# A two-layer step with routed experts on one core: the last three chunks' rows stay in SBUF and are placed by products, the further chunks run in pairs in the middle

## What is computed

```python
u = x * (1 + scale1) + shift1
y, k, v = token_mixer(u, p, lam_init, rope, ctx_kv)
x = layer_norm(ALPHA * x + gate1 * y, p['ln1_g'], p['ln1_b'])
u = x * (1 + scale2) + shift2
x = layer_norm(ALPHA * x + gate2 * hier_moe(u, p), p['ln2_g'], p['ln2_b'])
...
h = silu(einsum('nd,edf->nef', t, p['w_gate'])) * einsum('nd,edf->nef', t, p['w_up'])
y = einsum('nef,efd->nd', h * comb[:, :, None], p['w_down'])
```

## Time and profile before

| what | us |
|---|---|
| median of 3 runs (1164.85 to 1168.12) | 1165.8 |
| the profiled execution | 1164.11 |
| its span, first to last instruction | 1162.3 |
| PE busy | 928.0 |
| DVE busy | 368.5 |
| ACT busy | 234.0 |
| POOL busy | 172.4 |

### The profile page before, as it was taken

One profiled execution on the slowest core, in us unless ns is written; L12 is line 12 of the kernel. 1 busy time (PEld: TensorE's weight loads), 2 busy tenths in 40 slices (PEclk: granted clock), 3 DMA queues, 4 the chain that ended last, 5 costly groups with the idle time before them and its releaser, 6 DMA issues.

```text
span 1162.3 us, 13769 instructions
## 1 busy us (share of the span) xinstructions
PE 928.0 (80%) x5214; PEld 535.7 (46%) x5214; DVE 368.5 (32%) x887; ACT 234.0 (20%) x575; POOL 172.4 (15%) x203
## 2 busy tenths in 40 slices
PE   3899988984999877775789989898599887777542
PEld 2356455543555534342345546554455543433222
DVE  0158462154211111110547845116311111111052
ACT  1200265052111110111230036306011110101023
POOL 5000000002232222211020000000232222221100
PEclk8899989996999999999789999999799999999976
DMA  9962162266999999999932227038699999996521
GB/s 367 378 252 92 57 249 93 100 277 241 387 414 414 414 413 413 411 411 380 363 120 109 108 91 288 3 131 334 251 397 412 416 413 412 411 413 255 226 110 54
DMA packets 72831, 321.86 MB, mean 277 GB/s; under 512 B 12974, under 2 KB 17286, under 8 KB 48448
## 3 DMA queue, kind: packets, MB, share of 16 engines
q1 hardware_dynamic: 57680, 294.14, 63.5%
q0 software_dynamic: 14224, 20.57, 5.0%
q10 hardware_dynamic: 864, 6.29, 1.4%
HBM read 320.93 MB, written 23.59 MB: 296 GB/s over the span
## 4 chain that ended last, share of the span: by engine, by line
PE 53%; SPq 22%; DMA 12%; DVE 8%; issue 2%; ACT 2%; ACTq 0%; DVEq 0%; POOLq 0%; POOL 0%
PE ps L751 13%; PE ps L979 9%; SPq L541 8%; SPq L543 7%; PE ps L927 7%; SPq L548 6%; PE ps L994 4%; DMA arena<-in_w_up 4%; PE ps L754 4%; DMA ring<-in_w_mod 3%; PE ps L713 3%; DMA arena<-y_pairs 2%; PE ps L909 2%; PE ps L914 2%; PE ps L987 1%
## 5 line engine op out<-in xcount | busy, mean ns | idle before, releaser
L979 PE MATMUL ps<-ring,tail 128*64 128x256 f32 x1728 | 201.2, 385 | 35.3 <-DMA ring<-in_w_up 33.4
L979 PEld LDWEIGHTS ps<-ring,tail 128*64 128x64 f32 x1728 | 135.4, 139 | 115.8 <-DMA ring<-in_w_up 55.1
L751 PE MATMUL ps<-uT,ring 128*128 128x384 f32 x448 | 152.2, 497 | 8.5 <-ACT uT L1093 8.2
L1627 DVE TENSOR_TENSOR arena<-arena,ps 128x128 f32<-128x128 f32 x68 | 19.5, 287 | 382.6 <-ACT arena L1249 382.6
L751 PEld LDWEIGHTS ps<-uT,ring 128*128 128x128 f32 x448 | 86.3, 194 | 67.2 <-issue 11.0
L1249 ACT ACTIVATE arena<-ps 128x128 f32<-128x128 f32 x68 | 18.8, 277 | 484.9 <-PE ps L979 484.9
L646 POOL DMA_INDIRECT y_pairs<-tail,row_idx x64 | 64.6, 1009 | 341.6 <-PE ps L987 297.7
L994 PE MATMUL ps<-ring,krow 128*64 128x512 f32 x432 | 104.6, 601 | 2.6 <-issue 1.3
L641 POOL DMA_INDIRECT arena<-u_rows,row_idx x66 | 67.5, 1023 | 42.3 <-issue 20.0
L713 PE MATMUL ps<-ring,sT 128*32 128x512 f32 (+1 forms) x512 | 52.8, 555 | 21.0 <-DMA ring<-in_w_mod 21.0
L1379 DVE SCALAR_TENSOR_TENSOR arena<-arena,dw 128x414 f32<-128x414 f32 x118 | 67.6, 645 | 0.0
(11 more groups left out here) (243 smaller groups left out, 959.1 us busy)
## 6 DMA issues: line engine op xcount, KB each, us to landing
ring<-in_w_gate SPq DMA_DIRECT2D x54, 1024.0 KB, 17.8
ring<-in_w_up SPq DMA_DIRECT2D x54, 1024.0 KB, 23.6
ring<-in_w_down SPq DMA_DIRECT2D x54, 1024.0 KB, 23.5
ring<-in_w_mod SPq DMA_DIRECT2D x12, 3072.0 KB, 12.7
arena<-in_w_gate SPq DMA_DIRECT2D x14, 1024.0 KB, 17.6
arena<-in_w_up SPq DMA_DIRECT2D x14, 1024.0 KB, 23.2
arena<-in_w_down SPq DMA_DIRECT2D x14, 1024.0 KB, 23.5
ring<-in_w_mod SPq DMA_DIRECT2D x6, 2048.0 KB, 15.7
```

Source lines behind the costliest of these rows:

```text
L751: last = mm(ps[:, n % 4, 0:T], slot[s][:, k, c:c + P], uT[:, k, :], start=(k == 0), stop=(k == KD - 1))
L979: last = mm(ps[W * half:W * (half + 1), b, 0:2 * P].rearrange("p (j f) -> p j f", j=2), xc[:, b, k, :], gate_up_w[s][:, :, k, half * P:(ha ...
```

## The change

**Start.** Of the table of constants only the first 256 columns load ahead of everything; the rest loads behind the first projection slot.

**Further chunks in the middle.** 31 experts' chunks are unrolled. The 32nd expert's chunk and all further chunks form a list that runs in a loop after the first 20, two in a turn, on slots 3 and 4, with doubled buffers; the list is filled up to an even number. Then the other 11 chunks follow. The last chunks use slots 0 to 3 alone.

**The last three chunks** (28 to 30) are not scattered. Their rows in `y_pairs` are set to zero by three puts at the start of the stage; the rows of 28 and 29 are stacked in one tile, 64 partitions each (`down_stacked`), those of 30 stay in `yrow`. Placing matrices (row, token) that hold the routing weights are built by DVE and turned by PE before the first chunk (`late_places`). After chunk 30 `late_products` multiplies rows by placing matrices straight into the PSUM tiles from which z is made, and the sums of the pair rows are added onto them by products with the identity. POOL issues the loads of the pair rows when chunk 27 is stored.

**Norm.** The gain is applied in the scaling itself (`xT = centred * gain * 1/root`); the bias is folded into the modulation's shift (`mod_fold`) and into the next residual. `scale_x` of the second residual moves into chunks 20 to 27. Of the modulation products that follow a norm, two or three k-tiles move between the sums and the sums of squares; the next layer's first ones come after the norm.

```diff
+NS = NE - 1
+SPLIT = 20
+PLACE = [i if i < SPLIT else i + 2 for i in range(NS)]
+PUT = NS - 3
+SLOT_AT = [(FIRST_SLOT + p) % XRING for p in range(27)] + [0, 1, 2, 3, 1, 0]
...
-            sp.dma_start(cst[:], consts).then_inc(s_cst.sem, 16)
+            sp.dma_start(cst[:, 0:first], consts[:, 0:first]).then_inc(s_cst.sem, 16)
...
+                with sp.Fori(0, turns, 2) as r:
+                    for p in range(2):
...
+                        sp.wait_ge(e_gate_up.sem, before + (r + p + 1))
+                        load_gate_up(LOOP_SLOT[p], ds(e, 1), e_gate_up_loaded[p])
...
+                        sp.wait_ge(e_down.sem, before + (r + p + 1))
+                        load_down(LOOP_SLOT[p], ds(e, 1), e_down_loaded[p])
...
+                for i in range(PUT, NS):
+                    put(row_idx[:, CHUNKS + i:CHUNKS + i + 1], zero_rows, zeros_put)
...
+                    for p in range(2):
+                        pool.wait_ge(e_rows_loaded[p].sem, (before + (r + 2 * l + 4)) * 8)
+                        pool.wait_ge(e_stored[p].sem, (before + (r + 2)) * 8)
+                    pool.sem_inc(e_free.sem, 2)
+                for i in range(SPLIT + 2, SPLIT + 4):
+                    fetch_chunk(i)
...
+                for t in range(NT):
+                    pool.dma_start(yk[:, t, :], y_pairs.rearrange("(t q r) n -> t q (r n)", t=NT, r=4)[t]).then_inc(y_loaded[t].sem, 16)
...
+                        if which == 0:
+                            mod_product(l, 2, 7, range(2))
+                        elif l + 1 < DEPTH:
+                            mod_product(l + 1, 0, 7, range(MOD_K))
...
+                def down_stacked(b, c, s, sig):
+                    for f in range(2):
+                        for half in range(2):
+                            last = mm(ps[W * c:W * (c + 1), 3 + half, :], hT[:, b, f * W:(f + 1) * W],
+                                      down_w[s][:, f, half * 512:(half + 1) * 512],
+                                      start=(f == 0), stop=(f == 1), tile_position=(0, W * c))
...
+                def late_products(m):
+                    h, n = m // 4, m % 4
+                    mm(ps[:, n, 0:T], ystack[:, m * P:(m + 1) * P], late_place[:, 0, :], start=True, stop=False)
+                    mm(ps[:, n, 0:T], yrow[W * h:W * (h + 1), 0, n * P:(n + 1) * P], late_place[W * h:W * (h + 1), 1, :],
+                       start=False, stop=False)
+                wait(y_rows, l, NS)
+                for m in range(4):
+                    late_products(m)
                 wait(y_sum, l, NT)
                 for m in range(KD):
-                    if m >= 4:
-                        wait(z_ready, l, KD + m - 3)
                     for t in range(NT):
-                        last = tr(ps[:, m % 4, t * P:(t + 1) * P], ysum[:, t, m * P:(m + 1) * P], ident)
+                        last = mm(ps[:, m % 4, t * P:(t + 1) * P], yk[:, t, m * P:(m + 1) * P], ident,
+                                  start=False, stop=(t == NT - 1))
                     last.then_inc(y2_ready.sem, 1)
+                    if m + 4 < KD:
+                        wait(z_ready, l, KD + m + 1)
+                        late_products(m + 4)
                     if m >= 1:
                         layer_norm(1, m - 1)
                 layer_norm(1, KD - 1)
+                if l + 1 < DEPTH:
+                    mod_product(l + 1, 0, 7, range(MOD_K, KD))
+                    mod_turn(l + 1, 0, 6, 0)
...
+                wait(y_stored[0], l, SPLIT // 2)
+                wait(y_stored[1], l, SPLIT // 2)
+                with act.Fori(0, turns, 2) as r:
...
-                        v.tensor_tensor(uT[:, m, :], uT[:, m, :], ln_t[:, 0, :], ALU.mult).then_inc(normed.sem, 1)
+                        v.scalar_tensor_tensor(xT[:, m, :], uT[:, m, :], vcol(l, g0, m), ln_t[:, 0, :], ALU.mult,
+                                               ALU.mult).then_inc(normed.sem, 1)
```

More of the change, by code:

```diff
@@ L511, in _ @@
                 else:
-                    sp.wait_ge(e_down.sem, before + 1)
+                    wait(down_done, l - 1, NS, alone=True)
                 load_slot(0, [(slot[0][:, :, POOL:SLOT_COLS], cols(w_in, c0, c0 + 2 * CONV, 0, KD)),
@@ new lines, in _ @@
+                for i in range(SPLIT + 2, SPLIT + 4):
+                    fetch_chunk(i)
+                for i in range(SPLIT, PUT):
+                    if i + XBUFS < NS:
+                        wait(x_turned, l, i + 1, alone=True)
+                        fetch_chunk(i + XBUFS)
+                    put_chunk(i)
+                wait(y_stored[0], l, PUT // 2)
+                wait(y_stored[1], l, PUT // 2)
+                wait(zeros_put, l, 3)
+                wait(down_done, l, max(i for i in range(NS) if SLOT_OF[i] == RING) + 1, alone=True)
@@ new lines, in main_chunks @@
+                def main_chunks(first, end):
+                    main_x(first)
+                    main_x(first + 1)
+                    if first == 0:
+                        late_places()
+                    main_gate_up(first)
+                    for i in range(first, end):
+                        b = i % 2
+                        wait(h_ready, l, i + 1)
+                        wait(hT_ready, l, i - 1)
+                        tr(ps[:, 2 + 5 * b, 0:P], hrow[:, b, :], ident).then_inc(h_turned.sem, 1)
+                        if i + 2 < end:
+                            main_x(i + 2)
+                        s = SLOT_OF[i]
+                        wait(down_loaded[s], l, SLOT_USE[i])
+                        wait(hT_ready, l, i + 1)
+                        wait(y_rows, l, i if i >= PUT else i - 1)
+                        if i < 2:
+                            wait(late_ready, l, 2)
+                        if PUT <= i < NS - 1:
+                            down_stacked(b, i - PUT, s, down_done)
+                        else:
+                            down(b, s, down_done)
+                        if i + 1 < end:
+                            main_gate_up(i + 1)
@@ L1280, in _ @@
+                main_chunks(SPLIT, NS, turns)
+                squares_root(1)
                 if l + 1 < DEPTH:
                     mod_rows_out(l + 1, 0, 7)
-                squares_root(1)
-                new_x("ln2", 1, x_new, (l + 1, 1), SH1, SC1, u_act if l + 1 < DEPTH else None)
+                    new_u(1, (l + 1, 1), SH1, SC1, u_act)
+            for m in range(0, KD, 2):
+                wait(normed, DEPTH - 1, KD + m + 1)
+                fn(uT[:, m, :], xT[:, m, :], ID, bias=vcol(DEPTH - 1, "ln2_b", m)).then_inc(x_out.sem, 1)
@@ new lines, in _ @@
+                wait(h_turned, l, SPLIT)
+                with dve.Fori(0, turns, 2) as r:
+                    for p in range(2):
+                        dve.wait_ge(e_turned.sem, before + (r + (p + 1)))
+                        copy_x(p, e_copied)
+                    for p in range(2):
+                        dve.wait_ge(e_silu.sem, before + (r + (p + 1)))
+                        hidden(p, e_hidden)
+                        dve.wait_ge(e_hturned.sem, before + (r + (p + 1)))
+                        columns(p, e_columns)
@@ L1671, in _ @@
                 residual_norm(1)
-                new_x("ln2", 1, x_new_dve, (l + 1, 1), SH1, SC1, u_dve if l + 1 < DEPTH else None)
-                own.check()
+                if l + 1 < DEPTH:
+                    new_u(1, (l + 1, 1), SH1, SC1, u_dve)
+                    own.check()
+            for m in range(1, KD, 2):
+                wait(normed, DEPTH - 1, KD + m + 1)
+                v.tensor_scalar(uT[:, m, :], xT[:, m, :], vcol(DEPTH - 1, "ln2_b", m), None, ALU.add).then_inc(x_out_dve.sem, 1)
```

525 lines of the change are left out of this document (288 added, 237 removed).

## The result

The changed kernel takes 1181.7 us (median of 4 runs, 1179.8 to 1183.9) against 1165.4 before: a ratio of 1.0136, 95% interval 1.0118 to 1.0153. It is 16.3 us **slower**; 1164.2 was forecast, with a range to 1174. The profiled execution took 1182.6, its span is 1180.8.

The account below looks back on a forecast made before the run. Weights were taken to set the pace, 7.64 us a chunk. Start -2.5, norm -1.6, layer 0 +0.6 and layer 1 +1.9 sum to -1.6: 1164.2 us for the median, range 1150 to 1174.

Parts of the forecast that it names:

- rival B: Residual's stage: PE's waits for DVE in each tile drop the granted clock, +9 us a layer, 1182 us; chance 0.06.
- 22.0 for the stage: Residual's stage, first identity product to last sum of z: takes 22.0 us at full clock.
- Now all but hidden: Before layer 0's residual: pair rows' loads, 15.3 us, and sum end at 124.8, late products at 123.8; 15.9 us lay open before.
- The pace of the stream: Unrolled chunks: three weight loads, 3.146 MB at 412 GB/s, set a pace of 7.64 us a chunk.
- The loop: Middle loop: late fetch of chunk 22 stalls PE from about 32 to 41, leaving it 11 us behind the stream at chunk 30.
- ACT's hold: Loop's start: ACT waits for both y buffers, so the first chunk's SiLU runs 2 us late.
- Late products: After chunk 30: 0.66 us each with issue, eight ahead of the pair rows' sum taking 5.3 us.
- Start and norm: Start: fewer constants ahead of the modulation weights, -2.5 us; norm without separate gain and bias, -0.8 a layer, -1.6 together.
- Behind M both programs do about the same: After each layer's last sum of z, old and new kernels were taken to do about the same work.
- the same work: Norm: modulation products moved around the sums, their weights already in SBUF, lie only at another place; cost 0.
- rival C: Loop: weight stream runs dry with two slots, a chunk costing 12.94 us, adding 10 us, 1174 us; chance 0.13.
- A: Rival: stall behind the loop is short, landings below 5 us, 5.1 us less a layer, 1154 us; chance 0.28.

Follow-up runs that it names:

- e1: Changed kernel, with the next layer's three modulation loads issued only when the pair rows have landed; 1162.4 us, 0.9960 of the kernel before.
- e6: On top of e1, layer 1's pair rows load only behind the last down product; 1179.1 us, 1.0104 of the kernel before.
- e2: Changed kernel, with three k-tiles of modulation products moved ahead of PE's wait for the pair rows' sum; 1168.4 us, 1.0018 of the kernel before.
- e5: As e3 but without placing by products: all 31 chunks scattered, PE turns the sums as before; 1156.0 us, 0.9915 of the kernel before.
- b2: As e5, with the third modulation load held until the pair rows have landed; 1146.8 us, 0.9820 of the kernel before.
- e4: Changed kernel, with the second residual's sums of the previous tile put ahead of PE's wait for z; 1166.9 us, 1.0008 of the kernel before.
- e3: Changed kernel, with x rows of chunks 22 and 23 fetched by the loop's own last turn; 1169.3 us, 1.0021 of the kernel before.

## Why the prediction was wrong

The time came out as rival B, slower at 1182, to which I had given 6 in 100; the range ended below it. That B's figure fits is luck: B had both layers' stages at the low clock, for DVE's wait in each tile, +18. Only layer 0's fell, behind another wait, and the rest came from elsewhere. The profiled time missed by 20.1 us. Gains and losses against the kernel before, by stretch (chunk 19 stands for the start of its gate and up; start and norm of a layer are in the stretch ahead of its chunk 19):

| stretch | forecast | measured |
|---|---|---|
| up to chunk 19 of layer 0 | -3.3 | 0.0 |
| chunk 19 to M, layer 0 | +0.6 | +13.3 |
| M of layer 0 to chunk 19 of layer 1 | -0.8 | +6.2 |
| chunk 19 to M, layer 1 | +1.9 | -1.6 |
| behind M of layer 1 | 0 | +0.6 |

- **The step that failed** is "22.0 for the stage" in layer 0, with full clock taken for granted. In layer 1 the sum was right (22.8 measured). In layer 0 it took 34.9: 12.9 of the 20.1 us. Rows 16 had shown the low clock at this very place behind a wait of 3.08; against it I had argued that the clock came back there "with waits as short" and that PE "comes from dense work now". The waits were not as short: that stage of the kernel before has none above 0.3 us, the new one has 0.9 in four tiles. And PE did come from dense work, but the long wait still came between.
- **"Now all but hidden"**: my sum had the pair rows ready 1.0 us behind the late products. I put 15.3 us on their loads beside the modulation weights; they took 18.7, and PE stood 3.39. That a few us of lateness there would be paid several times over, I did not see: e1 and e6 show it from two sides, and e2's profiled execution from a third. (There is a slip in that sum too: 107.1 + 15.3 is 122.4, not 122.7.)
- **The pace of the stream** was too fast, 7.64 us a chunk; the gathered rows (0.26 MB a chunk) come over the same DMA engines as the weights, and 3.41/0.412 is 8.3. The profile of before has 8.2, in layer 0:

```profile
493.66 3.67 PE L979 MATMUL ps<-ring,tail 128*64 128x256 f32 x32 [1.14 <-DMA ring<-in_w_up]
501.87 3.67 PE L979 MATMUL ps<-ring,tail 128*64 128x256 f32 x32 [1.14 <-DMA ring<-in_w_up]
```

 Chunk 19 thus starts at 420.18 (420.14 before the change) and not at 426.7, and from there to the residual it takes 131.2 us and not 124.8. That the stage began at 551.34, where I had 551.5, is luck: the two errors cancel.
- **The loop** (4.0 of these 6.4 us, with the late products; the rest is the wait for the rows) was right in kind and short in size. ACT's hold cost 3.0 us (2 forecast) and one slow down product 1.65, which I had left out; chunk 22's turning stood 8.76 and 7.54 (8 to 9 forecast).
- **Late products** are 0.84 us apart, not 0.66: 1.4 us for the first eight. Why they are slower than the projections of the same columns was not tried.
- **Start and norm**: the gains came and went. The first projection starts 0.9 earlier and the router 1.0, but the first norm's last sum and the first chunk's gate and up stand where they stood. Timeline of the kernel after:

```profile
40.69 23.11 PE L822 MATMUL ps<-uT,ring 128*128 128x384 f32 x64 [1.67 <-ACT uT L1216]
...
252.83 4.71 PE L1018 MATMUL ps<-uT,router_w 128*36 128x384 f32 x14 [1.31 <-DVE uT L1456]
...
284.95 4.93 PE L1056 MATMUL ps<-ring,tail 128*64 128x256 f32 x32
```

 Against the earlier trace rows: 253.80 and 285.01. The placing matrices' turning (1.49 us) took back what the norm had given. Of -3.3 forecast up to there, nothing was left.
- **"Behind M both programs do about the same"** failed by 6.2 us. M to chunk 19 of layer 1 took 396.0. My numbers give 396.4 (969.9 - 573.5), but only because 7.64 a chunk puts chunk 19 too late in layer 1 as well; in the kernel before it took 389.7. Timeline of before, then of after:

```profile
586.00 1.62 PE L751 MATMUL ps<-uT,ring 128*128 128x384 f32 x2 [6.50 <-ACT uT L1093]
...
962.62 3.67 PE L979 MATMUL ps<-ring,tail 128*64 128x256 f32 x32 [1.16 <-DMA ring<-in_w_up]
```

```profile
586.12 2.78 PE L784 MATMUL ps<-ring,sT 128*32 128x512 f32 x24
...
594.20 4.50 PE L784 MATMUL ps<-ring,sT 128*32 128x512 f32 x40
...
602.66 23.72 PE L822 MATMUL ps<-uT,ring 128*128 128x384 f32 x64 [2.59 <-ACT uT L1216]
...
982.16 3.67 PE L1056 MATMUL ps<-ring,tail 128*64 128x256 f32 x32 [1.15 <-DMA ring<-in_w_up]
```

 The first projection (`L751`, `L822`) starts 13.1 us behind M before and 16.5 after. The modulation products (`L784`), which PE did before while it waited for the pair rows, now stand between the two; I had them at 0, as "the same work" at another place. e2, which does 24 of these 64 instructions ahead of the stage, has 15.0. Another 2.5 us are lost up to layer 1's first gate and up, ahead of which the placing matrices are turned; what they are made of was not tried.
- **Right**: the stream didn't run dry in layer 0's loop (rival C), and the landings behind the loop stayed long (against A).

The Trainium skill (TensorE: Matmul & The Clock Gate, "A second HAM failure mode: psum-queue depth-cycling") says that small idles between groups of products can make the clock swing. Here they did not do so alone: layer 1 and e1 kept 1.00 with the same idles. Behind a longer wait the low clock lasted 14 to 29 us with them and 8.5 with most of them filled; that they are what holds it is not shown.

## What to carry to other kernels

Where an edit turns a place that waits into one that works, look at the granted clock of that place before and ask which wait is left just ahead of it: a wait of 3 us in front of a stage with gaps cost up to 12 us more than itself. Another order of loads gave it back; products that fill the wait did so in the profiled run, not in every run. Work that was hidden in a wait costs its time when it is moved out of it. Price a transfer by all that shares the DMA engines in that moment, and hold what isn't needed yet behind what the critical engine waits for. And before a latency is replaced by computation, measure the latency without its contention: here holding back other loads gained 1.0% (e5 to b2), and the replacement gained nothing.

## Unexpected of the hardware

The same products in the same order ran at 0.50 for 29 us or at 1.00 throughout, by whether PE had waited 3.39 us (or 5.55, e6) or none ahead of them; with the short gaps filled the low clock lasted 8.5 us (e4), and 14 us in e3 with the gaps as they were. A wait of this length isn't always followed by the low clock: in layer 1's loop of the kernel before, a gate and up product took 5.36 us behind a wait of 3.55 and 3.67, as at full clock, behind one of 3.60; the prediction used only the first. Three 1 MB row loads took 18.7 us beside three modulation loads, 8.9 with those held back, and 9.6 in layer 1, where no other loads were left.
